# Expert stage of a hybrid encoder: all gate/up chunks in three fp32r passes, split weights double-buffered, the down remainder on GpSimd

## The chip, the cores and the metric

The kernel runs on one core of one Trainium2 chip. The metric is the device time of one execution in microseconds (us). Engines are named as the profile names them: PE is TensorE, PEld its weight loads, DVE is VectorE, ACT is ScalarE, POOL is GpSimd, SP is SyncE, which here only issues transfers. A name with q behind it (SPq, DVEq) is an engine's sequencer.

## What is computed

One layer of an encoder over 3072 tokens of width 1024: a mixer of two attention kinds, a hierarchical mixture of experts, a final norm. The change lies in the experts. There, tokens sorted by expert stand in blocks of 128, each block belonging to one expert:

```python
def run_block(args):
    tok, e = args
    xe = x[tok]                                        # 128 tokens x 1024
    hid = jax.nn.silu(xe @ w_gate[e]) * (xe @ w_up[e])  # 128 x 256
    return hid @ w_down[e]                             # 128 x 1024
yb = lax.map(run_block, (buf_tok.reshape(n_blocks, MOE_BLOCK), block_expert))
y = zeros.at[buf_tok].add(yb * buf_gate[:, None])
```

Each token goes to 2 of 32 experts, so there are at least 48 full blocks; with the padding of each expert to whole blocks, 64 blocks are live in this run, and 32 experts' weights (3 MB each in fp32) are loaded.

## The kernel before

The stages run one behind the other: projections, attention, output mix with router logits, `stage_route` (L1514, sorts tokens into blocks and writes into `eb`, for each block, its expert, whether the expert is new, and the slot of its weights), `stage_experts` (L1783), `stage_combine`. Only the route and expert stages are touched. In `stage_experts` every engine has its own program, and only semaphores tie them together. `over_blocks` (L1837) unrolls the first pair of blocks and then loops over pairs; `s` is the block's parity and picks one of two buffers.

For block b the work is this. POOL's `gather` (L1886) copies an index column (a cast, `cur`, L1888) and issues an indirect DMA that brings the 128 rows of x (L1891). PE's `x_turn` (L2016) transposes them, 8 times 128x128, into `psX`. Of the 8 chunks of the contraction, 4 (c = 4..7) are multiplied as plain fp32: DVE copies the transposed x (L1980), and PE multiplies it with the weights as loaded (L2051). The other 4 (c = 0..3) run in three passes of fp32r, hi·hi, hi·lo and lo·hi: ACT rounds x and weights to fp32r (`xT_hi` L1938, `wg_hi` L1934), DVE subtracts to get the remainders (`xT_lo` L1982, `wg_lo` L1988), and PE runs 12 matmuls (L2056). Gate and up lie side by side, so each matmul has 512 columns. ACT then takes silu of the gate half (L1968), DVE multiplies with the up half (`hid`, L2010), PE transposes it (`hid_turn`, L2025, L2029), ACT and DVE split it (`hT_hi` L1942, `hT_lo` L1993), and PE's `down` (L2032) runs 12 fp32r matmuls (L2040) with the split down weights (`wd_hi` on ACT, L1948; `wd_lo` on DVE, L2000). ACT scales the result by the gate (`y_out`: L1953, L1955), and POOL's `add` (L1896) waits for the add before it to land, casts the target indices (`to`, L1899), and issues an indirect DMA that adds the rows into H2 (L1904).

SP loads an expert's three weights (gate, up L1868, down L1870) into one of `WS` = 4 slots once the down product four blocks back is done, waits for all three to land, and then raises `w_ready` (L1874), for which ACT, DVE (through ACT) and PE wait.

PE's order in body b is: plain chunks of b, three-pass chunks of b, hid_turn(b-1), x_turn(b+1), down(b-1). ACT's is: wg_round(b), xT_round(b), y_out(b-2), wd_round(b), hT_round(b-1), silu(b). DVE's is: the copy of xT(b), xT_lo(b), wg_lo(b), wd_lo(b), hT_lo(b-1), hid(b). POOL alternates gather(b+4) and add(b). `wg_hi`/`wg_lo` have one buffer, `wd_hi`/`wd_lo` two.

Of the kernel before, what the change touches and what calls it, by code (L numbers as in the profile page):

```python
# [13 lines left out]
P = 128  # L14
# [25 lines left out]
DE = 256  # L40
# [1473 lines left out]
WS = 4  # L1514


def stage_route(nc, t, logits, eb, idx, gates):
# [3 lines left out]
    with ExitStack() as ctx:  # L1521
# [59 lines left out]
        ord_i = sb("ord_i", [1, BLOCKS], I32)  # L1581
        live_i = sb("live_i", [1, 1], I32)
# [42 lines left out]
        def _(dve):  # L1625
# [141 lines left out]
            nc.vector.tensor_scalar(eb[:, SLOT_AT:SLOT_AT + BLOCKS], ord_i[:, :], WS - 1, None, ALU.bitwise_and)  # L1767
# [16 lines left out]
def stage_experts(nc, t, eb, idx, gates):  # L1784
# [3 lines left out]
    with ExitStack() as ctx:  # L1788
# [67 lines left out]
        def _(sp):  # L1856
            sp.dma_start(ident[:, :], t["ident"]).then_inc(ident_loaded, 16)
            sp.sem_inc(y_psum, WS)

            def body(b, j, s):  # L1860
                new = sp.value_load(eb[0:1, bass.ds(b + NEW_AT, 1)], min_val=0, max_val=1)
                with sp.If(new > 0):
# [20 lines left out]
        def _(pool):  # L1883
            pool.sem_inc(xT_psum, 2)

# [36 lines left out]
            for k in range(2):  # L1922
                add(2 * pairs - 4 + 2 * k, 0, added + 16 * k)
                add(2 * pairs - 3 + 2 * k, 1, added + 16 + 16 * k)

        @block.scalar
        def _(act):
            act.sem_inc(y_landed, 2)

# [14 lines left out]
            def wd_round(b, s):  # L1944
# [3 lines left out]
                nc.scalar.activation(wd_hi[:, s * HC:(s + 1) * HC, :], w_dn[:, bass.ds(w * HC, HC), :], ACT.Copy).then_inc(wd_rounded, 1)  # L1948
# [21 lines left out]
            act.sem_inc(hid_ready, 1)  # L1970
# [6 lines left out]
        def _(dve):  # L1977
            def xT_out(b):
                dve.wait_ge(xT_psum, b + 3)
# [262 lines left out]
```

## Time and profile before

| | |
|---|---|
| Median of 3 runs | 4127.71 us (4121.14 to 4137.02) |
| The profiled execution | 4129.44 us, its span 4127.6 us |
| Mean granted TensorE clock | 0.952 |
| PE busy | 3739.1 us (91%) |
| PEld busy | 2729.3 us (66%) |
| DVE busy | 2763.0 us (67%) |
| ACT busy | 2377.5 us (58%) |
| POOL busy | 554.9 us (13%) |
| Expert stage | from about 3330 to 4062 us of the span |

The page names, for each group of instructions, the line, the engine, the operation, its tiles (output <- input), shapes and count, then the busy time, the mean duration, and the idle time of the engine before them with what ended it. Durations overlap on an engine: two matmuls of 0.39 us can start 0.23 us apart, so what a matmul costs is read from the distance of starts. On ACT and DVE the next instruction starts about 0.09 us before the end shown for the last one.

### The profile page before, as it was taken

Reading aid. Unit: us, or ns where it says so; the run is one execution under the profiler, and the core shown is the slowest. Engines: PE = TensorE matmul, PEld = TensorE weight load, DVE = VectorE, ACT = ScalarE, POOL = GpSimd, SP = SyncE. Lnnn points to the kernel's source line nnn. Section 1 sums busy time; section 2 is a strip of 40 time slices with the busy share of each in tenths; the row PEclk is TensorE's granted clock in tenths of the full one; section 3 lists DMA queues with packets and bytes.
Section 4 is the critical chain, followed back from the end, with each engine's and each line's share of the span. In section 5 each row is a group of like instructions: output and inputs, shape, how many; then the busy total and the mean of one; then the engine's idle time right before and its main releaser. Section 6 shows DMA issues by size and latency. Waiting matters only on the chain. (4 is left out here: it accounts for less than half of the span.)

```text
span 4127.6 us, 59990 instructions
## 1 busy us (share of the span) xinstructions
PE 3739.1 (91%) x16747; PEld 2729.3 (66%) x16748; DVE 2763.0 (67%) x4425; ACT 2377.5 (58%) x4123; POOL 554.9 (13%) x553
## 2 busy tenths in 40 slices
PE   7999948999999999999999999996999569999992
PEld 7888825666666666667667666764777456666661
DVE  5656547878878898878677777854343556666564
ACT  4443304777777777766676666676333135555554
POOL 0000000111111111110110111100000013333331
PEclk9999967999999999999999999998999889999996
DMA  4464570220222112221121122002333158888787
GB/s 164 153 218 160 189 187 16 61 54 20 56 62 61 44 33 52 61 61 26 41 60 42 25 61 49 16 7 90 137 129 135 53 169 240 239 244 251 230 239 270
DMA packets 308135, 454.66 MB, mean 110 GB/s; under 512 B 118230, under 2 KB 245490, under 8 KB 296850
## 3 DMA queue, kind: packets, MB, share of 16 engines
q1 hardware_dynamic: 241942, 359.85, 29.1%
q0 software_dynamic: 18576, 67.64, 6.9%
q10 hardware_dynamic: 47376, 24.26, 2.0%
q8 instruction: 115, 1.88, 0.2%
q14 instruction: 126, 1.03, 0.1%
HBM read 305.68 MB, written 146.05 MB: 109 GB/s over the span
## 5 line engine op out<-in xcount | busy, mean ns | idle before, releaser
L940 ACT ACTIVATE b_p_hi<-b_psS 128x512 fp32r<-128x512 f32 (+1 forms) x1376 | 822.0, 597 | 587.6 <-PE b_psS L1071 575.8
L1071 PE MATMUL b_psS<-b_q,b_k 96*128 96x512 f32 (+3 forms) x3440 | 1051.3, 403 | 24.7 <-issue 18.2
L988 DVE TENSOR_TENSOR b_p_lo<-b_prob,b_p_hi 128x512 fp32r<-128x512 f32 x1152 | 830.1, 722 | 252.3 <-ACT b_prob L943 207.1
L943 ACT ACTIVATE b_prob<-b_psS 128x512 f32<-128x512 f32 (+1 forms) x1376 | 815.0, 592 | 1.1
L1071 PEld LDWEIGHTS b_psS<-b_q,b_k 96*128 96x128 f32 (+3 forms) x3440 | 628.0, 186 | 255.9 <-issue 25.6
L996 DVE TENSOR_REDUCE b_mx_s<-b_psM 128x1 f32<-128x512 f32 x1024 | 691.5, 687 | 86.6 <-PE b_psM L1102 66.6
L1102 PE MATMUL b_psM<-b_k,b_q 128*128 128x512 f32 (+1 forms) x1280 | 516.1, 424 | 54.2 <-DMA b_v<-V 39.4
L1094 PE MATMUL b_psO<-b_p_hi,b_v_hi 128*65 128x512 f32 x1280 | 516.2, 403 | 26.3 <-DVE b_p_lo L988 24.4
L1094 PE MATMUL b_psO<-b_p_hi,b_v_lo 128*65 128x512 f32 x1280 | 509.5, 398 | 0.0
L1094 PE MATMUL b_psO<-b_p_lo,b_v_hi 128*65 128x512 f32 x1280 | 509.0, 398 | 0.0
L929 POOL TENSOR_TENSOR b_p_lo<-b_prob,b_p_hi 128x512 fp32r<-128x512 f32 x128 | 166.6, 1301 | 1684.8 <-ACT b_prob L943 1684.8
L1102 PEld LDWEIGHTS b_psM<-b_k,b_q 128*128 128x128 f32 (+1 forms) x1280 | 251.7, 197 | 157.5 <-DVE b_mx_s L996 52.4
L1094 PEld LDWEIGHTS b_psO<-b_p_lo,b_v_hi 128*65 128x65 f32 x1280 | 175.9, 137 | 125.3 <-issue 5.1
L1094 PEld LDWEIGHTS b_psO<-b_p_hi,b_v_hi 128*65 128x65 f32 x1280 | 176.6, 138 | 118.9 <-DVE b_p_lo L988 51.3
L1094 PEld LDWEIGHTS b_psO<-b_p_hi,b_v_lo 128*65 128x65 f32 x1280 | 177.2, 138 | 110.1 <-issue 4.0
L2051 PE MATMUL e_psG<-e_w_gu,e_xT 128*128 x512 | 233.2, 598 | 11.0 <-SPq L1874 10.0
L612 PE MATMUL a_psZ<-a_w_hi,a_xT_hi 128*128 128x396 f32 x600 | 209.4, 349 | 24.6 <-DVE a_w_lo L569 24.6
L612 PE MATMUL a_psZ<-a_w_hi,a_xT_lo 128*128 128x396 f32 x600 | 207.3, 345 | 0.0
L612 PE MATMUL a_psZ<-a_w_lo,a_xT_hi 128*128 128x396 f32 x600 | 206.5, 344 | 0.0
L996 DVE TENSOR_REDUCE b_mx_p<-b_psM 128x1 f32<-128x512 f32 x256 | 173.9, 687 | 30.7 <-PE b_psM L1102 27.6
L1934 ACT ACTIVATE e_wg_hi<-e_w_gu 128x2048 fp32r x64 | 122.7, 1917 | 106.5 <-SPq L1874 85.2
L2000 DVE TENSOR_TENSOR e_wd_lo<-e_w_dn,e_wd_hi 128x2048 fp32r<-128x2048 f32 x64 | 146.7, 2292 | 37.6 <-ACT e_wd_hi L1948 35.8
(247 smaller groups left out, 5274.9 us busy)
## 6 DMA issues: line engine op xcount, KB each, us to landing
e_w_gu<-w_gate SPq DMA_DIRECT2D x32, 1024.0 KB, 7.7
e_w_gu<-w_up SPq DMA_DIRECT2D x32, 1024.0 KB, 10.0
e_w_dn<-w_down SPq DMA_DIRECT2D x32, 1024.0 KB, 13.6
a_x_raw<-xallT SPq DMA_DIRECT2D x25, 512.0 KB, 5.0
a_x<-xall SPq DMA_DIRECT2D x25, 512.0 KB, 4.2
c_o<-O SPq DMA_DIRECT2D x24, 512.0 KB, 4.8
c_x<-xall SPq DMA_DIRECT2D x24, 512.0 KB, 3.6
H<-c_h SPq DMA_DIRECT2D x24, 512.0 KB, 2.7
```

What stands on the lines that cost most here:

```text
L612: i = nc.tensor.matmul(psZ[:, b, 0:ZW], xx[:, s, c, :], ww[:, c, b * ZW:b * ZW + ZW], start=n == 0, stop=n == 3 * KC - 1)
L929: nc.gpsimd.tensor_tensor(p_lo[:, slot, :], prob[0:kn, slot, :], p_hi[0:kn, slot, :].bitcast(F32), ALU.subtract).then_inc(lo_ready_pool, 1)
L940: nc.scalar.activation(p_hi[0:kn, (s * NI + j) % NP, :], psS[0:kn, j % 2, :], ACT.Exp)
L943: nc.scalar.activation(prob[0:kn, (s * NI + j) % NP, :], psS[0:kn, j % 2, :], ACT.Exp).then_inc(p_ready, 1)
L988: nc.vector.tensor_tensor(out, prob[0:kn, slot, :], p_hi[0:kn, slot, :].bitcast(F32), ALU.subtract).then_inc(lo_ready, 1)
L996: nc.vector.tensor_reduce(dst, psM[:, u % 2, :], AX.X, ALU.max).then_inc(m_free, 1)
L1071: m = nc.tensor.matmul(psS[0:kn, j % 2, :], kk[s][0:r, k], qq[s][0:r, q], start=n == 0, stop=n == len(passes) - 1)
L1094: m = nc.tensor.matmul(psO[0:VC, b % 2, :], vv[s][:, vc, :], pp[:, slot, :], start=first and n == 0, stop=last and n == 2)
L1102: nc.tensor.matmul(psM[:, u % 2, :], q0[s][0:r, q * P:q * P + P], k0[s][0:r, kc:kc + 512], start=True, stop=True).then_inc(m_psum, 1)
L1934: nc.scalar.activation(wg_hi[:, :, :], w_gu[:, bass.ds(w * KC, HK), :], ACT.Copy).then_inc(wg_rounded, 1)
L2000: nc.vector.tensor_tensor(wd_lo[:, c, :], w_dn[:, bass.ds(w * HC, HC), :], wd_hi[:, c, :].bitcast(F32), ALU.subtract).then_inc(wd_ready, 1)
L2051: nc.tensor.matmul(psG[:, s, :], xT[:, c - HK, :], w_gu[:, bass.ds(w * KC + c, 1), :].rearrange("p o n -> p (o n)"), start=c == HK, stop=F ...
```

## The change

1. All 8 chunks of gate/up run in three fp32r passes. `xT`, its copy on DVE and the plain matmuls are gone; `xT_hi`, `xT_lo` hold 8 chunks and two blocks, `wg_hi`, `wg_lo` 8 chunks and two blocks.
2. The split of the weights for block b+1 is done during block b, in 4 quarters (`NQ` = 4, two chunks each), with a semaphore step for each quarter on ACT, DVE and PE.
3. `wd_rest`, the down remainder, goes from DVE to POOL, in two halves (128x1024 each); `wd_round` on ACT is cut in the same halves, the second behind silu.
4. PE's order in body b is now x_turn(b+1), the first 12 matmuls of gate/up, hid_turn(b-1), the other 12, down(b-1). `hid` has one buffer.
5. Weight slots: 3 instead of 4 (the slot is the ordinal modulo 3, worked out in the route stage with a multiply and a shift). SP loads gate/up for b once DVE's remainders of block b-3 are done, and down once POOL's of b-3 are done, and still waits for all three.
6. POOL's order is gather(b+3), wd_rest(b), add(b-1). `logits` is freed before the experts.

The core of the diff:

```diff
-WS = 4
+WS = 3
@@ stage_route, vector
-            nc.vector.tensor_scalar(eb[:, SLOT_AT:SLOT_AT + BLOCKS], ord_i[:, :], WS - 1, None, ALU.bitwise_and)
+            nc.vector.tensor_scalar(third[:, :], ord_i[:, :], 171.0, None, ALU.mult)
+            dve.drain()
+            nc.vector.tensor_scalar(third[:, :], third[:, :], 9, None, ALU.arith_shift_right)
+            dve.drain()
+            nc.vector.scalar_tensor_tensor(eb[:, SLOT_AT:SLOT_AT + BLOCKS], third[:, :], -float(WS), ord_i[:, :], ALU.mult, ALU.add)
@@ stage_experts, tiles
-        xT = sb("xT", [P, KC - HK, P])
-        xT_hi, xT_lo = sb("xT_hi", [P, HK, P], F32R), sb("xT_lo", [P, HK, P], F32R)
-        wg_hi, wg_lo = sb("wg_hi", [P, HK, 2 * DE], F32R), sb("wg_lo", [P, HK, 2 * DE], F32R)
+        xT_hi, xT_lo = sb("xT_hi", [P, 2, KC, P], F32R), sb("xT_lo", [P, 2, KC, P], F32R)
+        wg_hi, wg_lo = sb("wg_hi", [P, 2 * KC, 2 * DE], F32R), sb("wg_lo", [P, 2 * KC, 2 * DE], F32R)
@@ sync, body
-                    sp.wait_ge(y_psum, b + 1)
+                    sp.wait_ge(wg_ready, NQ * b + NQ)
                     ... gate and up loads
+                    sp.wait_ge(wd_ready, HC * b + HC)
                     ... down load
@@ gpsimd
+            def wd_rest(b, s):
+                w = pool.value_load(eb[0:1, bass.ds(b + SLOT_AT, 1)], min_val=0, max_val=WS - 1)
+                for c in range(HC):
+                    pool.wait_ge(wd_rounded, HC * (b + 4) + c + 1)
+                    pool.sem_inc(pool_carrier, 1)
+                    nc.gpsimd.tensor_tensor(wd_lo[:, s * HC + c:s * HC + c + 1, :], w_dn[:, bass.ds(w * HC + c, 1), :],
+                                            wd_hi[:, s * HC + c:s * HC + c + 1, :].bitcast(F32), ALU.subtract).then_inc(wd_ready, 1)
                 with pool.If(j < pairs + 1):
                     gather(2 * j, j, 0)
+                    wd_rest(2 * j - 3, 1)
                 with pool.If(j < pairs):
                     add(2 * j - 4, 0, 16 * j - 32)
                     gather(2 * j + 1, j, 1)
+                    wd_rest(2 * j - 2, 0)
                     add(2 * j - 3, 1, 16 * j - 16)
@@ scalar, body
-                wg_round(b)
-                xT_round(b)
                 if not isinstance(b, int) or b > 1:
                     y_out(b - 2, j - 1, s)
-                wd_round(b, s)
+                if not is_last(b):
+                    xT_round(b + 1, 1 - s)
+                    wg_round(b + 1, 1 - s, 0)
+                wd_round(b, s, 0)
+                if not is_last(b):
+                    wg_round(b + 1, 1 - s, 1)
                 if not isinstance(b, int) or b > 0:
                     hT_round(b - 1)
+                if not is_last(b):
+                    wg_round(b + 1, 1 - s, 2)
+                    wg_round(b + 1, 1 - s, 3)
                 ... silu(b)
+                wd_round(b, s, 1)
@@ vector, body
-                xT_out(b)
-                wg_rest(b)
-                wd_rest(b, s)
+                if not is_last(b):
+                    xT_rest(b + 1, 1 - s)
+                    wg_rest(b + 1, 1 - s, 0)
                 if not isinstance(b, int) or b > 0:
                     hT_out(b - 1)
+                if not is_last(b):
+                    wg_rest(b + 1, 1 - s, 1)
+                    wg_rest(b + 1, 1 - s, 2)
                 ... hid(b)
+                if not is_last(b):
+                    wg_rest(b + 1, 1 - s, 3)
@@ tensor
-                pe.wait_ge(wd_ready, b + 1)
+                pe.wait_ge(wd_ready, HC * WS + HC * b + HC)
@@ tensor, body
-                for c in range(HK, KC):
-                    nc.tensor.matmul(psG[:, s, :], xT[:, c - HK, :], w_gu[...], start=c == HK, stop=False)
+                if not is_last(b):
+                    x_turn(b + 1, j + s, 1 - s)
+                pe.wait_ge(xT_rest_ready, 2 * b + 2)
+                for c in range(KC):
+                    if c % QK == 0:
+                        pe.wait_ge(wg_ready, NQ * WS + NQ * b + c // QK + 1)
+                    for k, (a, ww) in enumerate(((xT_hi, wg_hi), (xT_hi, wg_lo), (xT_lo, wg_hi))):
+                        i = nc.tensor.matmul(psG[:, s, :], a[:, s, c, :], ww[:, s * KC + c, :], start=c == 0 and k == 0,
+                                             stop=c == KC - 1 and k == 2)
+                    if c == KC // 2 - 1 and some_before:
+                        hid_turn(b - 1)
+                i.then_inc(g_psum, 1)
                 if some_before:
                     down(b - 1, 1 - s)
```

## Rows read from the trace of the kernel before

**Rows 1.** Source L1968 (silu), one per block: ns min/median/max, first and last start.

```profile
L1968 ACT ACTIVATE e_act_g<-e_psG x64: 378/379/385, 3358.2 to 4039.2; 128x256 f32<-128x256 f32 x64
```

**Rows 2.** Windows: us, then PE, PEld, DVE, ACT, POOL busy, PEclk, DMA share, GB/s.

```profile
3500.00:3600.00 100.00, 97.39 (x388) 66.34 (x387) 62.95 (x56) 58.10 (x67) 37.44 (x37) 1.00 0.86 254
3800.00:3900.00 100.00, 94.06 (x371) 64.48 (x371) 58.59 (x51) 54.18 (x63) 37.66 (x37) 0.98 0.81 237
```

**Rows 3.** Timeline of PE over one block: start us, duration us.

```profile
3435.87 3.59 PE L2051 MATMUL e_psG<-e_w_gu,e_xT 128*128 x8
...
3440.09 0.40 PE L2056 MATMUL e_psG<-e_wg_hi,e_xT_lo 128*128 128x512 f32 x1
...
3442.17 0.40 PE L2056 MATMUL e_psG<-e_wg_hi,e_xT_lo 128*128 128x512 f32 x1
3442.41 0.39 PE L2029 MATMUL e_psH<-e_ident,e_hid 128*128 128x128 f32 x2
...
3443.91 0.49 PE L2040 MATMUL e_psY<-e_wd_hi,e_hT_hi 128*128 128x512 f32 x1 [0.21 <-DVE e_hT_lo L1993]
```

**Rows 4.** By line, shapes apart, 3400 to 4000 us: busy us, mean ns, idle before.

```profile
L1955 ACT ACTIVATE e_y<-e_psY,e_gcur 128x1024 f32<-128x1024 f32 x55 | 61.3, 1115 | 3.8
L1938 ACT ACTIVATE e_xT_hi<-e_psX 128x512 fp32r<-128x512 f32 x56 | 32.3, 577 | 0.0
L1942 ACT ACTIVATE e_hT_hi<-e_psH 128x256 fp32r<-128x256 f32 x56 | 21.6, 386 | 185.9 <-PE e_psH L2029 185.9
```

**Rows 5.** Sources L1322 and L1366, the 128x1024 forms: ns min/median/max.

```profile
L1322 ACT ACTIVATE c_oT_hi<-c_oT x24: 1043/1059/1061, 2869.1 to 3220.6; 128x1024 fp32r<-128x1024 f32 x24
L1366 DVE TENSOR_TENSOR c_oT_lo<-c_oT,c_oT_hi x24: 1217/1218/1226, 2870.2 to 3221.9; 128x1024 fp32r<-128x1024 f32 x24
```

**Rows 6.** Timeline of POOL over one add and one gather: start us, duration us.

```profile
3517.51 0.18 POOL L1899 CAST e_to<-idx 128x1 uint32 x1 [7.20 <-DMA H<-e_y,e_to]
3518.64 1.60 POOL L1904 DMA_INDIRECT H<-e_y,e_to  x1 [0.94 <-POOL e_to L1899]
3519.68 0.76 POOL L1888 CAST e_cur<-idx 128x1 uint32 x1
3521.24 0.99 POOL L1891 DMA_INDIRECT e_x<-U,e_cur  x1 [0.80 <-POOL e_cur L1888]
```

**Rows 7.** By line, shapes apart, POOL, whole span: busy us, mean ns, idle before.

```profile
L916 POOL TENSOR_TENSOR b_v_lo<-b_v,b_v_hi 128x1040 fp32r<-128x1040 f32 x16 | 40.3, 2520 | 2.4 <-issue 0.2
```

**Rows 8.** Timeline in the attention stage, DVE and POOL at the same time.

```profile
1050.05 2.46 POOL L916 TENSOR_TENSOR b_v_lo<-b_v,b_v_hi 128x1040 fp32r<-128x1040 f32 x1
1050.14 2.92 DVE L988 TENSOR_TENSOR b_p_lo<-b_prob,b_p_hi 128x512 fp32r<-128x512 f32 x1 [0.21 <-issue]
...
1310.52 1.05 POOL L905 CAST b_v_hi<-b_v 128x1040 fp32r<-128x1040 f32 x1 [1.55 <-DMA b_v<-V]
1310.67 1.45 DVE L988 TENSOR_TENSOR b_p_lo<-b_prob,b_p_hi 128x512 fp32r<-128x512 f32 x1 [0.21 <-issue]
1311.71 2.72 POOL L916 TENSOR_TENSOR b_v_lo<-b_v,b_v_hi 128x1040 fp32r<-128x1040 f32 x1
```

**Rows 9.** Timeline in the expert stage, DVE and POOL at the same time.

```profile
3872.35 2.29 DVE L1988 TENSOR_TENSOR e_wg_lo<-e_w_gu,e_wg_hi 128x2048 fp32r<-128x2048 f32 x1 [0.19 <-issue]
3875.37 2.29 DVE L2000 TENSOR_TENSOR e_wd_lo<-e_w_dn,e_wd_hi 128x2048 fp32r<-128x2048 f32 x1 [0.73 <-ACT e_wd_hi L1948]
...
3872.44 2.24 POOL L1899 CAST e_to<-idx 128x1 uint32 x1 [1.64 <-DMA H<-e_y,e_to]
3875.63 3.50 POOL L1904 DMA_INDIRECT H<-e_y,e_to  x1 [0.95 <-POOL e_to L1899]
```

**Rows 10.** Source L2000, the down remainder on DVE: ns min/median/max.

```profile
L2000 DVE TENSOR_TENSOR e_wd_lo<-e_w_dn,e_wd_hi x64: 2284/2293/2321, 3354.3 to 4035.9; 128x2048 fp32r<-128x2048 f32 x64
```

**Rows 11.** Transfers, 3400 to 4000 us: KB each, median us from issue to landing.

```profile
e_w_dn<-w_down SPq DMA_DIRECT2D x27, 1024.0 KB, 13.7
H<-e_y,e_to POOLq DMA_INDIRECT x56, 8.8
```

More of the change, by code:

```diff
@@ L1581, in stage_route @@
         ord_i = sb("ord_i", [1, BLOCKS], I32)
+        third = sb("third", [1, BLOCKS], I32)
         live_i = sb("live_i", [1, 1], I32)
@@ L1799, in stage_experts @@
         HK = KC // 2
+        NQ = 4
+        QK = KC // NQ
         ident = sb("ident", [P, P])
@@ L1919, in _ @@
                     gather(2 * j + 1, j, 1)
+                    wd_rest(2 * j - 2, 0)
                     add(2 * j - 3, 1, 16 * j - 16)
             added = pool.value_load(eb[0:1, ADDED_AT:ADDED_AT + 1], min_val=16, max_val=16 * (BLOCKS // 2))
-            for k in range(2):
-                add(2 * pairs - 4 + 2 * k, 0, added + 16 * k)
-                add(2 * pairs - 3 + 2 * k, 1, added + 16 + 16 * k)
+            add(2 * pairs - 4, 0, added)
+            wd_rest(2 * pairs - 2, 0)
+            add(2 * pairs - 3, 1, added + 16)
+            wd_rest(2 * pairs - 1, 1)
+            for s in range(2):
+                add(2 * pairs - 2 + s, s, added + 16 + 16 * s)
         @block.scalar
@@ L1968, in body @@
                 nc.scalar.activation(act_g[:, :], psG[:, s, 0:DE], ACT.Silu).then_inc(silu_ready, 1)
+                wd_round(b, s, 1)
+            xT_round(0, 0)
+            for q in range(NQ):
+                wg_round(0, 0, q)
             act.sem_inc(hid_ready, 1)
@@ L1977, in _, with xT_rest, wg_rest @@
         def _(dve):
[L1978 to L1985 removed]
+            def xT_rest(b, s):
+                for k in range(2):
+                    dve.wait_ge(xT_rounded, 2 * b + k + 1)
+                    c = slice(k * HK, (k + 1) * HK)
+                    nc.vector.tensor_tensor(xT_lo[:, s, c, :], psX[:, k, :].rearrange("p (c n) -> p c n", n=P),
+                                            xT_hi[:, s, c, :].bitcast(F32), ALU.subtract).then_inc(xT_rest_ready, 1)
+            def wg_rest(b, s, q):
                 w = dve.value_load(eb[0:1, bass.ds(b + SLOT_AT, 1)], min_val=0, max_val=WS - 1)
[L1987 to L1988 removed]
+                dve.wait_ge(wg_rounded, NQ * b + q + 1)
+                c = slice(s * KC + q * QK, s * KC + (q + 1) * QK)
+                nc.vector.tensor_tensor(wg_lo[:, c, :], w_gu[:, bass.ds(w * KC + q * QK, QK), :], wg_hi[:, c, :].bitcast(F32),
                                         ALU.subtract).then_inc(wg_ready, 1)
@@ L2023, in x_turn, with hid_turn @@
                 i.then_inc(xT_psum, 1)
-            def hid_turn(b, s):
+            def hid_turn(b):
                 pe.wait_ge(hid_ready, b + 2)
-                hv = hid[:, s, :].rearrange("p (m c) -> p c m", c=HC)
+                hv = hid[:, :].rearrange("p (m c) -> p c m", c=HC)
                 for c in range(HC):
@@ L2045, in body @@
             def body(b, j, s):
-                w = pe.value_load(eb[0:1, bass.ds(b + SLOT_AT, 1)], min_val=0, max_val=WS - 1)
-                pe.wait_ge(w_ready, b + 1)
-                pe.wait_ge(xT_ready, b + 2)
-                for c in range(HK, KC):
-                    nc.tensor.matmul(psG[:, s, :], xT[:, c - HK, :], w_gu[:, bass.ds(w * KC + c, 1), :].rearrange("p o n -> p (o n)"), start=c == HK, stop=False)
-                pe.wait_ge(xT_rest_ready, b + 1)
-                pe.wait_ge(wg_ready, b + 1)
-                for c in range(HK):
-                    for a, ww in ((xT_hi, wg_hi), (xT_hi, wg_lo), (xT_lo, wg_hi)):
-                        i = nc.tensor.matmul(psG[:, s, :], a[:, c, :], ww[:, c, :], start=False,
-                                             stop=c == HK - 1 and ww is wg_hi and a is xT_lo)
-                i.then_inc(g_psum, 1)
                 some_before = not isinstance(b, int) or b > 0
-                if some_before:
-                    hid_turn(b - 1, 1 - s)
                 if not is_last(b):
                     x_turn(b + 1, j + s, 1 - s)
+                pe.wait_ge(xT_rest_ready, 2 * b + 2)
[8 more added lines that the diff above has]
+                i.then_inc(g_psum, 1)
                 if some_before:
                     down(b - 1, 1 - s)
-            pe.sem_inc(xT_ready, 1)
             pe.sem_inc(y_ready, 4)
@@ L2071, in _ @@
             pairs = over_blocks(pe, body)
-            hid_turn(2 * pairs - 1, 1)
+            hid_turn(2 * pairs - 1)
             down(2 * pairs - 1, 1)
```

56 lines of the change are left out of this document (30 added, 26 removed).

## Prediction, made before the changed kernel ran

> **What bounds the kernel now.** I read first how long a block takes. Silu runs once a block; its first start is at 3358.2 us and its last at 4039.2 us [rows 1], so 63 steps take 681.0 us, 10.81 us a block, and that is what the change can move: 681 us of the 4127.6 us span. Second, the windows: PE is busy 97% of a steady 100 us, ACT 58%, DVE 63%, POOL 37%, and the clock is at its 2.4 GHz level throughout [rows 2]. So PE bounds the stage, with no long wait in it. Third, the timeline of one block says what PE does [rows 3]. The 10 matmuls' starts from 3435.87 to 3440.09 are the 8 plain ones and two fp32r ones; nine fp32r steps from 3440.09 to 3442.17 take 2.08 us, 0.231 us each. The plain part is thus 4.22 - 2 x 0.231 = 3.76 us for 4 chunks, 0.94 a chunk; three fp32r passes cost 0.69 a chunk. From hid_turn at 3442.41 to the down product at 3443.91 is 1.50 us, of which 0.21 is a wait for `hT_lo`.
>
> **PE after the change.** Removed: 3.76 us of plain matmuls. Added: 12 fp32r matmuls, 12 x 0.231 = 2.77 us. The wait of 0.2 us goes if `hT_lo` comes earlier. PE's own work is 24 x 0.231 = 5.54 for gate/up, 12 x 0.231 = 2.77 for down, 1.28 for the ten transposes and 0.2 for steps between groups: 9.8 us a block. If nothing else took longer, the gain would be 63 x (10.81 - 9.8) = 64 us.
>
> **ACT.** Its 128x1024 copy takes 1.06 us [rows 5], 0.97 from start to start. It now has six (four quarters of `wg_hi`, two halves of `wd_hi`): 5.8 us. Two `xT_hi` of 0.577 make 1.0, y_out 1.115 with its gate copy 1.3, hT_hi 0.3 [rows 4], silu 0.4 with 0.3 behind it for the slot's register load. The sum is 9.1 us, close behind PE. Of its instructions, wd_round(b) half 0 and two quarters now stand ahead of hT_round(b-1). Laid out from the end of down(b-2): y_out to 1.5, xT_hi to 2.5, quarter 0 to 3.5, half 0 to 4.4, quarter 1 to 5.4, hT_hi to 5.8, hT_lo on DVE to 6.2; PE needs it at 1.0 + 5.54 + 0.25 = 6.8. It is covered by 0.6 us, and ACT is not the bound.
>
> **DVE.** Four remainders of 1.218 us (1.13 from start to start) [rows 5], two of 128x512 at about 0.6 by half that shape, and two small ones: 6.4 us. The down remainder, 2.29 us [rows 10], has left it.
>
> **POOL.** This is the step on which I bet. POOL gets two tensor_tensor of 128x1024. The nearest row is 128x1040: 2.46 us in one instance [rows 8], 2.52 in the mean [rows 7]; I take 2.42 each, 4.84 us. Its other work does not shrink: the add is a cast of 0.18, 0.95 to the indirect DMA, and 1.60 for that; the gather 0.18, 0.80 and 0.99 [rows 6]. That makes 2.73 + 1.97 + 4.84 = 9.54 us, with some 0.3 between instructions 9.9 us in one queue, alone as long as PE's 9.8.
>
> But it is not alone. In the attention stage a DVE tensor_tensor of 128x512 with both inputs in SBUF, for which half of a 128x1024 one's 1.22 us [rows 5] and a little more would do, starts at 1050.14, just behind a POOL one, and ends at 1053.06; POOL's ended at 1052.51 [rows 8]. DVE did nothing until POOL was done. At 1310.67 the same behind a POOL cast takes 1.45, and POOL's next instruction then takes 2.72 and not 2.46: DVE went in between. In the expert stage POOL is the loser: a cast of 0.18 us takes 2.24, ending with DVE's `wg_lo` at 3874.64, and an indirect DMA of 1.60 takes 3.50, ending 1.47 behind DVE's remainder [rows 9]. The other way round, DVE's `wd_lo` never took more than 2.321 us [rows 10], with 64 of POOL's indirect DMAs about. So POOL's tensor_tensor stops DVE's two-SBUF-input instructions, these stop anything that POOL starts, and the two take turns. The change puts 4 x 1.13 = 4.5 us of such work on DVE and 4.8 on POOL in each block. Operations with one input in PSUM (`xT_lo`, `hT_lo`, `hid`) are outside of it.
>
> How much of DVE's 4.5 us falls on POOL's chain? Nothing, if all four quarters fall into the 4.3 us of POOL's gaps and running DMAs; all 4.5, if each holds POOL up. I laid one period out with the durations above. A quarter is waiting when POOL's first half ends, and goes between the halves (+1.1); another waits when the second half ends, and holds the cast of `to` (+1.1); the other two run beside the add, whose start is held by 0.1 us. Sum: 9.9 + 2 x 1.1 = 12.1 us a block, the last 0.1 within its rounding. The bounds are 9.9 (none) and 14.4 (all); two quarters, give or take one, is 11.0 to 13.2.
>
> The Trainium skill ("SBUF — State Buffer", section "SBUF: two separate sides") says that DVE and GpSimd share a port pair under an exclusive lock, held for a whole instruction, and that a DVE operation with two SBUF inputs takes part in it against a GpSimd operation that reads SBUF. By that rule, the trace agrees, the one engine waits with nothing done. "GPSIMD Engine Reference", section "Engine selection", in the Trainium skill, advises VectorE for elementwise work, GpSimd being about twice as slow with two inputs; the rows have 2.46 against 1.22 us, and agree.
>
> PE in this case waits at down(b-1) for the remainder, some 2.3 us a block. One window with waits of that kind shows a clock of 0.98 where the others have 1.00 [rows 2]: 2 us at the 1.2 GHz level, 1 us of work lost. Even 2 us lost in each block would leave PE at 11.8, under POOL's 12.1.
>
> **Weights.** The down load of block b now starts when POOL has finished b-3. From issue to landing it took 13.7 us behind gate and up [rows 11]; alone, a third of that at least, 5 to 6. The chain POOL(b-3), load, ACT's body b-1 (7.5), ACT's body b (10.5), POOL(b) 2.4 is 26 to 35 us over three blocks, 8.8 to 11.7 a block: hidden behind 12.1, not behind 9.8. The add that must land before the next one took 8.8 us [rows 11], hidden too. The route stage gets two small instructions more, under 1 us. At the head, PE waits for the first quarter's split, but the plain matmuls are gone: 0 +- 3. At the tail, POOL's backlog of one half and one add puts 2 us.
>
> **Sum.** 63 x (12.1 - 10.81) = 81, plus 2 for the tail: 4129.4 + 83 = 4212 us. The profiled execution lies 1.7 us above the median of the three runs, less than they spread.
>
> **Rivals.** *PE stays the bound* (faster): DVE's quarters fall into POOL's gaps and POOL's 9.9 sets the pace with PE: 63 x 0.91 = 57 less, 4129.4 - 57 + 2 = 4074 us. For it: 4.3 us of POOL's time tolerate DVE. Against it: a half holds the port for 2.4 us, and DVE has work in most stretches of that length. 0.15. *One quarter caught a block* (no change): 11.0 us, 4129.4 + 63 x 0.2 + 2 = 4144 us. For it: the quarters are bunched around hid. 0.12. *The weights' chain* sets the pace, POOL's interference being small: 11.7 at most, 4188 us. 0.05; slower as well. *More than two caught*, or indirect DMAs drawn out at each start [rows 9]: 13.2 us, 4282 us. 0.08. *POOL bound with two caught*, the forecast: 0.60, from 11.6 to 12.7 us, 4180 to 4250 us. It becomes a loss as soon as POOL's chain is over 10.8, that is from 0.9 us of interference on.
>
> **Chances.** A measurement of this kernel can tell about 0.5%, 21 us, from no change. Slower 0.60 + 0.08 + 0.05 = 0.73. Within 0.5%: 0.12. Faster: 0.15. The range reaches down over the one-quarter rival and up over part of the heavy one: 4100 to 4262.
>
> **What would show it.** Right: POOL busy over 85% in the stage's windows, `wd_lo` on POOL with a mean over 2.6 us, `wg_lo` on DVE with a maximum over 3 us, PE's wait in front of L2040 released by POOL, silu every 12.1 us. Wrong: `wg_lo` always 1.22, PE without gaps and silu every 9.8 (first rival); ACT's `wg_hi` waiting for SP (weights).

## The result and the profile after

The changed kernel takes 4208.69 us (median of 4 runs, 4202.55 to 4213.95); the kernel before took 4125.83 us on the same chip (4121.14 to 4137.02). The ratio is 1.019, with a 95% interval of 1.0168 to 1.0212: slower by 83 us. The forecast was 4212 us, from 12.1 us a block.

The profiled execution of the changed kernel took 4202.6 us with a span of 4200.8. Silu comes first, the row that answers to [rows 1]:

```profile
L2006 ACT ACTIVATE e_act_g<-e_psG x64: 366/392/403, 3357.6 to 4111.8; 128x256 f32<-128x256 f32 x64
```

63 steps take 754.2 us, 11.97 us a block where it was 10.81. That is 73.2 us more, and the two spans differ by 4200.8 - 4127.6 = 73.2 us: head (3357.6 against 3358.2) and tail (89.0 us behind the last silu against 88.4) are unchanged, so the whole loss lies in the blocks' pace. It is 73 us here and 83 between the medians, because the profiled execution of the changed kernel is the fastest of its four and that of the kernel before lies 3.6 us above its median.

The windows, in the columns of [rows 2]:

```profile
3500.00:3600.00 100.00, 87.82 (x388) 70.46 (x388) 73.21 (x67) 72.44 (x103) 80.68 (x50) 0.93 0.76 218
3800.00:3900.00 100.00, 86.23 (x380) 69.28 (x380) 74.44 (x64) 69.96 (x99) 79.56 (x50) 0.91 0.78 226
```

PE fell from 97% and 94% busy to 88 and 86, its clock from 1.00 and 0.98 to 0.93 and 0.91; the DMA engines have less to do than before (0.77 against 0.84). POOL rose from 37% to 80. No engine shows 100%, so the bound has to be read from the waits (engine, the work that waited, whom it waited for, us in total, times, longest), 3450 to 4050 us:

```profile
PE e_psY L2085 <- POOL e_wd_lo L1925: 75.2, 43, 2.9
POOL H L1917 <- POOL e_to L1912: 44.6, 47, 1.0
POOL e_x L1904 <- POOL e_cur L1901: 40.6, 50, 0.8
POOL e_wd_lo L1925 <- issue: 30.3, 49, 1.1
POOL H L1917 <- issue: 4.2, 2, 2.3
POOL e_to L1912 <- issue: 0.2, 1, 0.2
```

PE waits for POOL's remainder in 43 of 50 blocks. POOL waits for nobody else: of its 120 us of idle time all but 4.4 are the 0.95 us between its own cast and its own indirect DMA, 0.8 us of the same kind at the gather, and the register load ahead of the remainder, and those 4.4 end with no other engine either (the last two rows). Before, `to`'s cast waited for the landing of an add, 7.2 us in [rows 6]; that wait is gone. POOL's queue is full at 80% busy.

One period of POOL, and DVE beside it (start us, duration us):

```profile
3716.96 5.72 POOL L1925 TENSOR_TENSOR e_wd_lo<-e_w_dn,e_wd_hi 128x1024 fp32r<-128x1024 f32 x2 [0.54 <-issue]
3722.62 1.18 POOL L1912 CAST e_to<-idx 128x1 uint32 x1
3724.75 1.62 POOL L1917 DMA_INDIRECT H<-e_y,e_to  x1 [0.95 <-POOL e_to L1912]
3725.82 0.74 POOL L1901 CAST e_cur<-idx 128x1 uint32 x1
```

```profile
3717.90 2.55 DVE L2031 TENSOR_TENSOR e_wg_lo<-e_w_gu,e_wg_hi 128x1024 fp32r<-128x1024 f32 x1 [0.47 <-ACT e_wg_hi L1962]
3720.37 0.41 DVE L2036 TENSOR_TENSOR e_hT_lo<-e_psH,e_hT_hi 128x256 fp32r<-128x256 f32 x1
3720.80 4.09 DVE L2031 TENSOR_TENSOR e_wg_lo<-e_w_gu,e_wg_hi 128x1024 fp32r<-128x1024 f32 x2
```

The first quarter starts at 3717.90 and is held until POOL's first half ends, one half (2.41 us) after 3716.96; it then runs its 1.1 us, and the second half starts behind it, so the two halves take 5.72 us and not 4.8. The next quarter starts at 3720.80, waits until the second half ends at 3722.68, and the cast of `to`, 0.18 us in [rows 6], takes 1.18: it waits for the quarter. Those are the two turns of the forecast, in the two places named.

Most blocks are like this one: of the 42 pairs of halves between 3500 and 4000 us 36 take about 5.7 us, and six take 4.8. One of the six is in the period before it:

```profile
3704.65 4.79 POOL L1925 TENSOR_TENSOR e_wd_lo<-e_w_dn,e_wd_hi 128x1024 fp32r<-128x1024 f32 x2 [0.25 <-issue]
3709.37 1.19 POOL L1912 CAST e_to<-idx 128x1 uint32 x1
3711.51 1.95 POOL L1917 DMA_INDIRECT H<-e_y,e_to  x1 [0.95 <-POOL e_to L1912]
3712.90 1.71 POOL L1901 CAST e_cur<-idx 128x1 uint32 x1
```

Here no quarter was waiting at the boundary between the halves (4.79). One held the cast of `to` as before (1.19), one the add's start (1.95 for 1.60) and one the cast of `cur` (1.71 for 0.74). The turn between the halves moved, and the sum stayed near 2 us: 2.3 here, 2.0 in the period shown first.

### The profile page after: what moved, and what is told of

It is laid out like the page before. It is cut to its first block and busy times, and to the rows that moved or that the text cites. A ratio compares the mean times of both kernels' runs of the same rounds, so it can differ in the third digit from the quotient of the medians.

```text
span 4200.8 us, 63405 instructions
## 1 busy us (share of the span) xinstructions
PE 3729.1 (89%) x17003; PEld 2799.8 (67%) x17003; DVE 2922.7 (70%) x4561; ACT 2535.2 (60%) x4449; POOL 919.8 (22%) x682
## 5 line engine op out<-in xcount | busy, mean ns | idle before, releaser
L2031 DVE TENSOR_TENSOR e_wg_lo<-e_w_gu,e_wg_hi 128x1024 fp32r<-128x1024 f32 x260 | 464.0, 1805 | 49.6 <-ACT e_wg_hi L1962 37.2
L1925 POOL TENSOR_TENSOR e_wd_lo<-e_w_dn,e_wd_hi 128x1024 fp32r<-128x1024 f32 x128 | 360.2, 2840 | 47.8 <-issue 35.7
L1962 ACT ACTIVATE e_wg_hi<-e_w_gu 128x1024 fp32r x260 | 268.1, 1060 | 9.9 <-SPq L1885 9.7
L2085 PE MATMUL e_psY<-e_wd_hi,e_hT_hi 128*128 128x512 f32 x256 | 126.9, 496 | 103.4 <-POOL e_wd_lo L1925 91.1
L2100 PE MATMUL e_psG<-e_wg_hi,e_xT_hi 128*128 128x512 f32 x512 | 211.8, 414 | 6.2 <-DVE e_wg_lo L2031 6.2
```

Of the source, the lines that this page charges most:

```text
L1925: nc.gpsimd.tensor_tensor(wd_lo[:, s * HC + c:s * HC + c + 1, :], w_dn[:, bass.ds(w * HC + c, 1), :], wd_hi[:, s * HC + c:s * HC + c + 1, ...
L1962: nc.scalar.activation(wg_hi[:, s * KC + q * QK:s * KC + (q + 1) * QK, :], w_gu[:, bass.ds(w * KC + q * QK, QK), :], ACT.Copy).then_inc(wg ...
L2031: nc.vector.tensor_tensor(wg_lo[:, c, :], w_gu[:, bass.ds(w * KC + q * QK, QK), :], wg_hi[:, c, :].bitcast(F32), ALU.subtract).then_inc(wg ...
L2100: i = nc.tensor.matmul(psG[:, s, :], a[:, s, c, :], ww[:, s * KC + c, :], start=c == 0 and k == 0, stop=c == KC - 1 and k == 2)
```

## Experiments

The theory under test: GpSimd's queue sets the pace, and it is over PE's 9.8 us only through turns with DVE's four quarters. The rivals: PE with its waits and its lost clock, the weights' chain through SP and the three slots, or the shape of GpSimd's work itself. Each kernel is the changed one with the edit shown. Times are medians, ratios are to the kernel before on the same chip; "a block" is the distance of the first and the last silu over 63. First the accounting that they are measured by, POOL by line, 3500 to 4000 us (busy us, mean ns, idle before), after:

```profile
L1925 POOL TENSOR_TENSOR e_wd_lo<-e_w_dn,e_wd_hi 128x1024 fp32r<-128x1024 f32 x84 | 234.8, 2816 | 25.2 <-issue 25.2
L1917 POOL DMA_INDIRECT H<-e_y,e_to x41 | 68.7, 1676 | 39.9 <-POOL e_to L1912 38.0 <-issue 1.9
L1912 POOL CAST e_to<-idx 128x1 uint32 x41 | 48.3, 1179 | 0.2 <-issue 0.2
L1901 POOL CAST e_cur<-idx 128x1 uint32 x41 | 36.3, 884 | 0.0
```

### e2: DVE's quarters take one input from PSUM

```diff
-nc.vector.tensor_tensor(wg_lo[...], w_gu[...], wg_hi[...].bitcast(F32), ALU.subtract)
+nc.vector.tensor_tensor(wg_lo[...], psZ[...], wg_hi[...].bitcast(F32), ALU.subtract)   # psZ: PSUM, zeros
```

> The changed kernel, but DVE's wg_lo subtracts wg_hi from a bank of zeros in PSUM instead of from the weights: the same count, shape and length of DVE instructions, with one input in SBUF and not two (the remainders of the gate/up weights are left out of the computation). POOL's work is untouched. My theory: DVE's wg_lo no longer takes turns with POOL, is 1.2 us each time, POOL's halves are 2.4 us, and POOL's queue alone takes 9.9 us plus the 0.6 us of register loading seen in front of its halves in the changed kernel: 10.5 us a block, 4129 - 63 x 0.3 = 4110 us, between 4090 and 4130. Rival, POOL's queue is too long whatever DVE does, or weights, or PE's clock: 4200 to 4215 us as the changed kernel.

Measured: 4101.24 us, ratio 0.9926 (0.9904 to 0.9948), 10.31 us a block: 107 us less than the changed kernel, with the same instructions, sizes and order on every engine; only where one input of four DVE instructions lies has changed. The mean of these four falls from 1.81 to 1.22 us. POOL by line, same columns:

```profile
L1926 POOL TENSOR_TENSOR e_wd_lo<-e_w_dn,e_wd_hi 128x1024 fp32r<-128x1024 f32 x96 | 229.0, 2411 | 21.6 <-issue 21.0 <-ACT e_wd_hi L1980 0.2
L1918 POOL DMA_INDIRECT H<-e_y,e_to x48 | 76.7, 1599 | 47.9 <-POOL e_to L1913 43.7 <-issue 4.2
L1902 POOL CAST e_cur<-idx 128x1 uint32 x48 | 35.7, 744 | 0.0
L1913 POOL CAST e_to<-idx 128x1 uint32 x47 | 8.8, 187 | 23.7 <-DMA H<-e_y,e_to 23.6
```

The differences of the means are the price of the turns: 2 x (2.816 - 2.411) = 0.81, the cast of `to` 1.179 - 0.187 = 0.99, the add 0.08, the cast of `cur` 0.14. Together 2.0 us a block; 11.97 less 2.0 is 10.0. `to`'s cast waits for landings again (23.6 us in 47 blocks, 0.5 a block), and the gap ahead of the remainder is 0.15 us shorter; with these the sum comes to e2's 10.3.

### e1: the down remainder back on DVE, everything else as changed

```diff
 vector, body
+                wd_rest(b, s, 0)          # behind wg_rest(b + 1, 1 - s, 0), ahead of hT_out(b - 1)
 ...
+                wd_rest(b, s, 1)          # last in the body
 gpsimd
-    two tensor_tensor of 128x1024 a block
```

> The changed kernel with one part undone: the down remainder wd_rest goes back to DVE (half 0 ahead of hT_lo, half 1 at the end of the body), POOL has its old work only; three passes, quarters, three slots, order of PE and of SP all stay. My theory (POOL's queue with its two tensor_tensor and the turns with DVE sets the pace): DVE's sum is 6.4 + 2.3 = 8.7 us a block, ACT's 9.1, PE's 9.8, so PE bounds again and silu comes every 9.8 to 10.1 us: 4129 - 63 x 0.9 = 4072 us, between 4060 and 4090. Rival, the three weight slots with the late down load: it stays over 4150 us, and ACT's wg_hi waits for SP. Rival, PE's lower clock (0.92 in the stage) or ACT's cut pieces: over 4150 us too.

Measured: 4111.49 us, ratio 0.9962 (0.995 to 0.9973), 10.43 us a block. The placement of one remainder is worth 97 us, and without it the rest of the change is a gain, if only of 16 us: e1 beats both kernels. But e1 was expected at 4060 to 4090 and missed it. PE is not the bound: of 450 us it is busy 421, while the DMA share is 0.86 (columns of [rows 2]), and several waits end with transfers:

```profile
3500.00:3950.00 450.00, 420.91 (x1993) 338.42 (x1991) 387.61 (x433) 373.85 (x521) 189.20 (x174) 0.99 0.86 251
```

```profile
POOL e_to L1912 <- DMA H<-e_y,e_to: 182.5, 44, 6.7
DVE e_wg_lo L2026 <- ACT e_wg_hi L1957: 34.8, 44, 9.2
ACT e_wg_hi L1957 <- SPq L1885: 19.1, 14, 8.8
PE e_psX L2070 <- DMA e_x<-U,e_cur: 9.1, 12, 2.8
```

ACT waits up to 8.8 us for SP's word that the weights are there, and PE for gathers. This opened a second question, what holds e1; it is taken up behind e7.

### e4: eight of the 24 gate/up matmuls left out

```diff
-for k, (a, ww) in enumerate(((xT_hi, wg_hi), (xT_hi, wg_lo), (xT_lo, wg_hi))):
+for k, (a, ww) in enumerate(((xT_hi, wg_hi), (xT_hi, wg_lo), (xT_lo, wg_hi))[:3 if c < HK else 1]):
```

> The changed kernel with 8 of the 24 gate/up matmuls left out (the two remainder passes of chunks 4 to 7 are not computed); all rounding and subtracting stays. It takes 8 x 0.231 = 1.85 us of PE's work out of each block. My theory, POOL's queue: no change against the changed kernel, 4209 us, within 10. Rival, PE at the lower granted clock is what lengthens the block: at least 63 x 1.85 = 117 us less, 4092 us; half of it if it shares the bound.

Measured: 4211.71 us, ratio 1.0203 (1.0184 to 1.0222), 12.00 us a block. A third of PE's gate/up work is gone and nothing is won; the clock fell further, to 0.90 in 3500 to 3900 us, and nothing is lost. Neither PE's work nor its clock sets the pace.

### e5: no weight loads in the loop

```diff
-    sp.dma_start(w_gu[...], ...) x2, sp.dma_start(w_dn[...], ...), wait for the landing     # each block
+    three slots loaded once, ahead of the loop
```

> The changed kernel with the weights of three experts loaded once ahead of the first block and no expert loads after that (29 of 32 loads are left out, the waits of SP's body stay). My theory, POOL's queue sets the pace: 4209 us less nothing, plus up to 10 for the 9 MB ahead of the first block, between 4200 and 4225. Rival, the weights' chain over three slots sets it: the block falls from 12 to about 10 us and the time to 4100 us.

Measured: 4236.03 us, ratio 1.0253 (1.0232 to 1.0274). The blocks take 12.20 us, no less than with the loads, though 1.5 MB of a block's 2.6 MB is gone. So the chain of the weights is not the cause. The time came out above the expected 4200 to 4225. The loads ahead of the loop make the first silu 18 us later, at 3375.7; the kernel before took 4133 us on this chip and not 4126; and the blocks are 0.2 us longer. POOL's own rows hold that 0.2: the gap ahead of the remainder is 34.7 us in 40.5 blocks, 0.86 and not 0.61 a block, the halves' mean is 2.875 and not 2.816, and the cast of `cur` is 0.12 shorter. Why the gap grew stays open.

### e3: one remainder of 128x2048 instead of two halves

```diff
-for c in range(HC): ... nc.gpsimd.tensor_tensor(wd_lo[:, s * HC + c:s * HC + c + 1, :], ...)
+nc.gpsimd.tensor_tensor(wd_lo[:, s * HC:(s + 1) * HC, :], ...)
```

> The changed kernel, but POOL subtracts the down remainder in one 128x2048 instruction instead of two of 128x1024, waiting for both halves of wd_hi. My theory: between the halves DVE takes a turn of 1.1 us in nearly every block; with one piece this turn is gone from POOL's queue: 12.1 - 1.1 = 11.0 us a block, 4209 - 63 x 1.1 = 4140 us, between 4130 and 4165. Rival, POOL's durations are just long (no turns): only 0.15 us a block for one instruction less, 4200 us.

Measured: 4213.02 us, ratio 1.0205 (1.0186 to 1.0224), 12.01 us a block. This is a miss: with no boundary between halves one turn should have gone, and 70 us with it. POOL by line shows where it went:

```profile
L1924 POOL TENSOR_TENSOR e_wd_lo<-e_w_dn,e_wd_hi 128x2048 fp32r<-128x2048 f32 x41 | 189.5, 4623 | 20.7 <-issue 20.7
L1917 POOL DMA_INDIRECT H<-e_y,e_to x42 | 82.5, 1964 | 40.9 <-POOL e_to L1912 39.0 <-issue 1.9
L1901 POOL CAST e_cur<-idx 128x1 uint32 x42 | 70.4, 1677 | 0.0
L1912 POOL CAST e_to<-idx 128x1 uint32 x41 | 47.7, 1163 | 0.9 <-DMA H<-e_y,e_to 0.9
```

The remainder runs undisturbed in 4.62 us. But the quarter held by it pushes the later ones back (in the timeline one starts at 3700.39 beside the remainder, takes 4.73 us, and the next two follow from 3705.37), and these now meet the small instructions: the cast of `to` 0.98 above its time in e2, the add 0.37, the cast of `cur` 0.93, 2.3 us in all. A turn taken away at one boundary came back at the next.

### e14: four remainders of 128x512

```diff
 for c in range(HC):
-    nc.gpsimd.tensor_tensor(wd_lo[..., c, :], ...)
+    for n in range(2):   # halves of the columns
+        nc.gpsimd.tensor_tensor(wd_lo[..., c, cols], ...)
```

> The changed kernel with POOL's down remainder in four pieces of 128x512 instead of two of 128x1024. One piece gave 4213 us where a turn less was to give 4140, so the turns are not tied to the gaps between pieces. Theory as it stands now, DVE's held time is conserved and shows up wherever POOL stands: only the fixed part of two more POOL instructions, 2 x (1.30 - 1.21) plus up to 0.15 each between them, 0.2 to 0.5 us a block: 4220 to 4240 us. Rival, each gap between pieces lets a quarter of 1.1 us in: 63 x 1.1 more at least, 4278 us or above.

Measured: 4301.67 us, ratio 1.0405 (1.0377 to 1.0433), 13.45 us a block, above the expected 4220 to 4240. POOL's timeline of one block and two of its means:

```profile
3704.90 6.99 POOL L1927 TENSOR_TENSOR e_wd_lo<-e_w_dn,e_wd_hi 128x512 fp32r<-128x512 f32 x4 [0.89 <-issue]
3711.84 1.18 POOL L1912 CAST e_to<-idx 128x1 uint32 x1
```

```profile
L1927 POOL TENSOR_TENSOR e_wd_lo<-e_w_dn,e_wd_hi 128x512 fp32r<-128x512 f32 x148 | 252.9, 1739 | 28.7 <-issue 28.7
L1917 POOL DMA_INDIRECT H<-e_y,e_to x37 | 68.4, 1850 | 37.6 <-issue 20.5 <-POOL e_to L1912 17.1
```

A POOL tensor_tensor of 128x512 takes 1.303 us in the mean of 128 in the attention stage, so four quarters of the remainder carry 4 x (1.739 - 1.303) = 1.74 us of turns, the cast 0.99, the add 0.25: 3.0 us of turns a block, one us more than in the changed kernel. With 0.4 us more for POOL's own work (four of 1.303 for two of 2.411) that makes 13.4 us. The rival of the expectation, 4278 us or above, is what came: more boundaries let more of DVE's quarters in. Held time is not conserved, then, and it is not one turn for each gap either, as e3 showed.

### e13: only two of DVE's four quarters read PSUM

```diff
+whole = psZ[...] if q % 2 else w_gu[...]
-nc.vector.tensor_tensor(wg_lo[...], w_gu[...], ...)
+nc.vector.tensor_tensor(wg_lo[...], whole, ...)
```

> The changed kernel with quarters 1 and 3 of DVE's wg_lo subtracting from zeros in PSUM (their remainders are left out of the computation), quarters 0 and 2 with both inputs in SBUF. Half the dose of the kernel in which all four read PSUM (4101 us, against 4209 for none). My theory, turns cost POOL what DVE holds: half of the 2.0 us of waits in POOL's queue stays, 11.0 us a block and 4155 us, between 4135 and 4180. Rival, one particular quarter does it all: the time is either by 4209 or by 4105.

Measured: 4176.95 us, ratio 1.0109 (1.0086 to 1.0132), 11.54 us a block. Within what was expected, near the upper end of the range: taking all four out of the sharing saves 107 us, taking two out saves 32. The rows say why: the remainder's mean is still 2.810 us and the cast's 1.043. In e13's timeline the quarters that hold POOL, between the halves and ahead of the cast, are the first and the third, and these still read SBUF; the second reads PSUM and takes its 1.21 us while one of POOL's halves runs (at 3621.51). Turns are paid by the quarter that happens to wait when a POOL instruction ends, not in proportion to DVE's work.

### e7: one half of the remainder on each engine

```diff
 gpsimd:  -for c in range(HC)   +c = 0 only
 vector:  +wd_rest(b, s, 1)      # last in the body
```

> The changed kernel with half 0 of the down remainder on POOL and half 1 on DVE, at the end of its body. My theory as the runs so far leave it (the turns with DVE are not tied to a place; they add some 2 us to POOL's chain when POOL and DVE are both filled, and DVE loses as much): POOL's own sum falls to 10.2 - 2.5 = 7.7 us, and with 2 us of turns it is at 9.7 at most; DVE has 7.5 us of work and waits up to 2.4. So POOL sets the pace no more and the kernel comes out by the down-on-DVE kernel, 4111 us, between 4095 and 4140. If instead any tensor_tensor on POOL costs in proportion to nothing (a fixed penalty of mixing the engines): over 4170 us.

Measured: 4117.07 us (4102.28 to 4130.04), ratio 0.9959 (0.9938 to 0.9979), 10.68 us a block. One POOL half fits: its mean is 2.595 us, turns are still paid, but POOL again has time to wait for landings. It gives what e1 gives.

### What holds e1: e10, e6, e9, e12

e10 is e1 with the loads out of the loop, as in e5.

> The kernel with the down remainder on DVE (e1, 4111 us), and no expert loads after the first three. In e1 a block takes 9.6 us in some stretches and 9.4 and 11.4 in turn in others, where ACT's wg_hi waits for the weights. Theory A, transfers (late weights, and a queue of transfers that slows the gathers and adds) make the 11.4: all blocks take 9.6 us, 4111 - 63 x (10.43 - 9.6) = 4059 us, with up to 10 more for the loads ahead of the first block. Theory B, the engines' own work makes it: 4111 us.

Measured: 4077.73 us, ratio 0.9866 (0.9846 to 0.9886), and 9.68 us a block although the first silu comes 31 us later than in e1. The clock is 1.00 and PE busy 447 of 450 us:

```profile
3500.00:3950.00 450.00, 447.09 (x2133) 362.37 (x2132) 406.26 (x464) 395.90 (x559) 212.56 (x186) 1.00 0.53 108
```

This is PE's floor, and it settles that the weight loads hold e1 above it, by 0.75 us a block. The same edit was worth nothing in e5: there POOL came first.

e6 is e1 with the add to `H` replaced by a plain indirect store:

```diff
-pool.indirect_dma_start(t["H2"], ..., y[:, s, :], None, compute_op=ALU.add)
+pool.indirect_dma_start(t["H2"], ..., y[:, s, :], None)
```

> The kernel with the down remainder on DVE (e1, 4111 us), where the indirect DMA of y writes its rows and does not add to them (the sum over experts is left out); it still waits for the one before to land. Theory A2, the chain of adds sets e1's pace: landing falls from 8.1 us to about 6.8 as the gathers have it, and the time by 30 us or more, to 4060 to 4085. Theory A1, the weights do: 4100 to 4111 us.

Measured: 4065.31 us, ratio 0.9841 (0.982 to 0.9862), 9.79 us a block. Queue q0 carries adds and gathers; its rows of e1 and of e6, 450 us each (packets, MB, share of 16 engines):

```profile
q0 software_dynamic: 12440, 45.26, 41.3%
```

```profile
q0 software_dynamic: 13246, 48.24, 29.2%
```

The add moves no more bytes by this count than the store, but takes 0.413 x 10.43 - 0.292 x 9.79 = 1.4 us more of all 16 DMA engines' time a block. With all the loads in, 268 GB/s go through, against e1's 251. Two things changed at once, though: the engines' time, and the serial chain of one add behind the landing of the last (cast 0.53, 0.9 to the add, landing 8.1: 9.5 of e1's 10.4 us). These runs do not tell the two apart. Nor is the packets' time a fixed price: in e10, with the same adds and gathers and no weight loads, q0 has a share of 52.6%, 5.1 us a block.

e9 and e12 are e1 with SP reporting gate/up and down apart, so that ACT can split gate/up sooner. e9 issues the down load only when gate/up has landed, e12 issues it right behind gate/up:

```diff
 sync, body
     gate/up: two dma_start, each with a semaphore of its own
+    wait for both; sp.sem_inc(gu_ready, 1)          # e9: here. e12: behind the issue of the down load
     wait for wd_ready; dma_start(w_dn)
     wait for its landing; sp.sem_inc(w_ready, 1)
```

> The kernel with the down remainder on DVE (e1, 4111 us), and the readiness of the weights split: ACT's wg_hi waits for gate and up alone, and only wd_hi waits for the down weights, whose load SP issues when gate and up have landed. Theory A1, the late down load holds back wg_hi of each new expert by about 1 us and with it PE by up to 1.8: half of the 31 slow blocks' 1.8 us at least, 4111 - 28 to 4111 - 50: 4061 to 4083 us. Theory A2, adds that wait for each other's landing set the pace (8.1 us of landing, 0.95 and 0.56 in front of it): 4105 to 4115 us as e1.

Measured: 4241.53 us, ratio 1.0261 (1.0239 to 1.0283), 12.54 us a block, where 4115 at most was expected. ACT's waits for SP, 3500 to 4000 us:

```profile
ACT e_wg_hi L1965 <- SPq L1883: 73.9, 17, 12.0
```

SP now does the transfers of each new expert one after the other, down behind gate/up, and ACT waits up to 12.0 us for it: a word that came sooner for one transfer made the next one start later. e12, which differs from e9 in this alone, takes 113 us less.

> The kernel with the down remainder on DVE (e1, 4111 us), with gate/up ready on their own as in the split-readiness kernel (4241 us), but all three loads are issued as early as in e1: SP issues the down load before it waits for gate and up. Theory: in the split kernel it was the serial issue (down only behind the landing of gate and up, the next expert behind that) that cost 130 us, and in e1 it is the down load, issued a block later than gate/up, that holds back wg_hi in every second block. Then this kernel has neither: 4065 to 4085 us. Rival: transfers are slow by their mere sum (weights, gathers and adds together at 255 GB/s), and readiness changes little: 4100 to 4111 us.

Measured: 4128.17 us, ratio 0.9988 (0.9971 to 1.0005), 10.73 us a block, another miss. Median us from issue to landing, in e1 and then in e12:

```profile
e_w_dn<-w_down SPq DMA_DIRECT2D x21, 1024.0 KB, 10.4
H<-e_y,e_to POOLq DMA_INDIRECT x44, 8.1
```

```profile
e_w_dn<-w_down SPq DMA_DIRECT2D x21, 1024.0 KB, 12.8
H<-e_y,e_to POOLq DMA_INDIRECT x41, 9.7
```

The same bytes in the same queues land later, adds included. In e1 SP waits 75.9 us in all (of 450) for DVE's remainder before it issues the down load, in e12 18.7: the down load now stands closer behind gate/up. That this makes the landings late is argued and not shown; no run separates it.

## Why the prediction was right, point by point

**What bounds the kernel after.** Right. The choice that carried the forecast was POOL's queue over PE's, and e2 and e1 show it from two sides: out of the sharing, 107 us less; off POOL, 97 us less. "PE stays the bound" is refuted by e4, "the weights' chain" by e5. ACT and DVE did not bound either, as forecast: of PE's waits between 3450 and 4050 us 6.6 end with `hT_lo`, against 75.2 with POOL's remainder.

**The number.** 4212 against 4208.7 us is closer than its parts. Against the profiled execution after, 4202.6 us, the forecast is 10 us too high: 8 from the pace (12.1 for 11.97 us, 63 times) and 2 from head and tail. The median lies 6 us above that execution, and that brings the two within 3 us; this part is luck.

**POOL's own work, 9.9 us.** The measured base is 11.97 - 2.0 = 10.0. The half of 2.42 was 2.41. The "0.3 between instructions" was 0.6 ahead of the remainder (25.2 us in 41 blocks), where its register load sits, but the whole is 0.1 over the forecast, so the rest of the queue has less than was allowed.

**Two turns of 1.1.** Right in the sum (2.0 for 2.2), and in the place for most of the blocks: 0.81 between the halves in the mean (0.9 in 36 of 42 pairs), 0.99 ahead of `to`'s cast, and 0.22 at the add and the cast of `cur`, where the forecast had 0.1. The forecast laid out one period as if all were alike, and POOL's are nearly so: its remainders start at 3693.00, 3704.65, 3716.96 and 3729.14, 11.7 to 12.3 us apart. The silus are not: they alternate between about 10.7 and 13.3 us, and only their mean is 12. The unevenness is PE's, not POOL's. The granted clock is lower at every second down product (four windows of 4 us, columns of [rows 2]):

```profile
3698.00:3702.00 4.00, 3.17 (x9) 2.56 (x10) 4.00 (x4) 0.85 (x1) 3.05 (x4) 0.70 0.76 235
3710.00:3714.00 4.00, 3.02 (x14) 2.42 (x14) 4.00 (x6) 2.16 (x3) 3.05 (x3) 1.00 0.80 260
3722.00:3726.00 4.00, 3.20 (x9) 2.51 (x10) 4.00 (x4) 1.00 (x2) 3.05 (x4) 0.69 0.96 327
3734.00:3738.00 4.00, 3.04 (x15) 2.49 (x15) 4.00 (x4) 2.14 (x3) 3.05 (x3) 1.00 0.35 121
```

A product at the lower clock takes 1.4 us longer (next point), and the silu behind it comes at a distance of 13.3 us and the one behind that at 10.9: 12 plus and minus about 1.3. The down products themselves start evenly, at 3698.83, 3711.09, 3722.80 and 3735.01. That this fits is read from the trace; no run changed the clock alone.

**"Nothing if all four quarters fall into gaps, all 4.5 if each holds POOL up."** The bounds were sound, but e3, e13 and e14 show that the number of turns cannot be changed at will inside them: one or two pieces, two turns; four pieces, three; two of DVE's four quarters out of it, still 1.7 us.

**PE.** 12 fp32r matmuls for 8 plain ones, and 9.8 us a block: e10 has 9.68 with PE 99% busy. Its waits at the down product were estimated at 2.3 us a block; the trace has 75.2 us in 50 blocks, 1.5, and clock loss beside it (the three rows are the first, the fifth and the sixth matmul of one down product):

```profile
3722.80 0.49 PE L2085 MATMUL e_psY<-e_wd_hi,e_hT_hi 128*128 128x512 f32 x1 [2.05 <-POOL e_wd_lo L1925]
...
3724.12 0.63 PE L2085 MATMUL e_psY<-e_wd_lo,e_hT_hi 128*128 128x512 f32 x1
3724.54 0.63 PE L2085 MATMUL e_psY<-e_wd_hi,e_hT_lo 128*128 128x512 f32 x1
```

PE was idle for 2.05 us ahead of the first row. The next three steps take 0.2 to 0.3 us each, and from 3723.69 on PE runs for 3 us at the 1.2 GHz level: 0.43 us from matmul to matmul, not 0.23. Seven such steps lose 1.4 us. Behind an idle time of 0.98 us, at 3711.09, the steps stay at 0.23. The loss is inside the 2 us allowed, and hidden behind POOL, as e4 confirms. The forecast's reading of the window at 0.98 was too small by half, though: a mean of 0.98 over 100 us is 4 us at the 1.2 GHz level and 2 us lost, not 2 and 1 (the trace has eight steps of 0.43 us from 3863.28 on, 1.6 us lost, behind an idle time of 2.01 us). Its sum does not use it.

**Weights, adds.** "Hidden behind 12.1, not behind 9.8" held both ways: e5 shows the first half, e1 against e10 the second. What the forecast left without a price is that second half. Its rival with PE as the bound put the change without POOL's trouble at 4074 us; the two runs nearest to that case, e2 and e1, have 4101 and 4111. In e1 the missing term is the transfers' 0.75 us a block (10.43 against e10's 9.68). The answer was not touched by it, because POOL hid it.

**Head and tail.** 2 us were given to the tail, which measured 0.6, and 0 to the head, which measured -0.6.

**Signs named.** The remainder's mean over 2.6 (2.840 over all 128), PE's wait released by POOL, silu at 12 us: seen. `wg_lo` has a mean of 1.805 us and single ones of 3.48:

```profile
L2031 DVE TENSOR_TENSOR e_wg_lo<-e_w_gu,e_wg_hi 128x1024 fp32r<-128x1024 f32 x260 | 464.0, 1805 | 49.6 <-ACT e_wg_hi L1962 37.2
```

"POOL busy over 85%" was wrong: it is 80. The sum of 12.1 us contains 1.8 us a block between a cast and its indirect DMA, and 0.6 at the register load, which the profile does not count as busy; (11.97 - 2.4) / 11.97 is 0.80. The threshold should have been worked out from the same sum as the time.

## What to carry to other kernels

Before work moves to GpSimd, write down which of DVE's instructions read both inputs from SBUF while it runs, and count one whole DVE instruction for each boundary between GpSimd instructions at which one can be waiting; splitting the work finer added boundaries here (e14, 93 us), and joining it only moved the turns to the next cast (e3). When one input came from PSUM the turns vanished (e2), and such a run tells whether the sharing was the cause. An engine can be saturated at 80% busy: look for waits on anything but itself, not for the percentage.

## What the runs showed of the hardware

A turn has a cost of its own kind for each instruction of GpSimd. A cast or a tensor_tensor waits with nothing done: the cast of `to` takes 1.18 us for 0.18, until DVE's quarter is done. An indirect DMA is held only at its start: in the timeline of 3704.65 the add starts at 3711.51, 0.4 us ahead of the end of a running quarter, and takes 1.95 us where 1.60 is its time alone; once it runs, DVE's next quarter goes on beside it, two in 2.34 us. That fits the 3.50 us of [rows 9] (2.03 until DVE's remainder ends, and 1.60, within 0.13) and the 2.321 us that DVE's remainder never exceeded in [rows 10]: no row shows DVE held by an add or a gather that already ran.

The Trainium skill ("SBUF — State Buffer", section "SBUF: two separate sides") has the two engines under an exclusive lock, held for a whole instruction. e2, e3 and the timelines agree for tensor_tensor and casts, each held to the end of the other's instruction; for an indirect DMA once it runs they do not, as told above. That a DVE operation with one PSUM input is outside of it was part of the forecast, and e2 shows it at 107 us.

With all loads and adds in, the highest rates over 3500 to 3950 us were 251 GB/s (e1) and 249 (e2), at DMA shares of 0.86 and 0.85; without the accumulation (e6) 268 GB/s went through at 0.80. Whether 251 is a limit was not tested.
